# Decaying the samples' SSD states on ScalarE instead of GpSimd, in a one-core hybrid decoder step

## The reference, cut to what matters

```
dA_cs  = dt * A
state' = exp(dA_cs) * state  +  (dt * x)[p] * B[n]      # new state, an output (ssm_sample)
y[p]   = sum over n of state'[p, n] * C[n]              # goes on into the mixer's output
```

## Time and profile before

| | |
|---|---|
| median of three runs | 2261.55 us (2261.43 to 2262.20) |
| the profiled execution, its own time | 2264.14 us |
| the profiled execution, its span in the trace | 2262.4 us |
| PE busy | 2144.6 us, 95% of the span |
| DVE busy | 1173.7 us, 52% |
| ACT busy | 848.9 us, 38% |
| POOL busy | 126.5 us, 6% |
| mean granted clock of PE | 0.976 of full speed |

### The profile page before, as it was taken

How to read it: one execution, slowest core, us unless ns; L and a number is a source line. 1 busy time by engine, 2 the same in 40 slices (tenths; PEclk the granted TensorE clock), 3 DMA queues, 4 the chain that set the end, 5 groups by cost and what they waited for, 6 DMA issues and landing times.

```text
span 2262.4 us, 39108 instructions
## 1 busy us (share of the span) xinstructions
PE 2144.6 (95%) x17101; PEld 1972.2 (87%) x17101; DVE 1173.7 (52%) x1582; ACT 848.9 (38%) x1031; POOL 126.5 (6%) x146
## 2 busy tenths in 40 slices
PE   5699999999999999989988899999999999999997
PEld 1188999988999999889988898899999989999996
DVE  1454444444444445576788877444545434445555
ACT  0143333333333333355655443333333323333333
POOL 0000000000000000011567000000000000000000
PEclk9799999999999999999999999999999999999998
DMA  9988865778888657757454456865545688875552
GB/s 388 402 301 311 307 236 191 240 270 305 307 309 313 225 183 273 266 168 216 153 171 143 154 183 224 294 228 185 170 158 180 213 303 315 309 264 168 160 177 85
DMA packets 380761, 534.10 MB, mean 236 GB/s; under 512 B 11815, under 2 KB 356783, under 8 KB 357807
## 3 DMA queue, kind: packets, MB, share of 16 engines
q1 hardware_dynamic: 358288, 519.28, 66.2%
q10 hardware_dynamic: 22303, 12.33, 1.9%
HBM read 524.37 MB, written 7.19 MB: 235 GB/s over the span
## 4 chain that ended last, share of the span: by engine, by line
PE 81%; DMA 8%; DVE 7%; ACT 2%; issue 1%; POOL 1%; SPq 1%; ACTq 0%; DVEq 0%; POOLq 0%
PE main L1365 25%; PE main L1366 24%; PE main L1367 24%; DMA ada<-in_w_ada 7%; PE b L1329 6%; DVE w_lo L847 2%; DMA ada<-in_w_ada_f 1%; DVE ntile L903 1%; ACT w_hi L577 1%; DVE h_lo L898 0%; SPq L439 0%; PE b L1314 0%; DMA raw<-in_w_in 0%; DVE rec L1161 0%; POOL state L540 0%
## 5 line engine op out<-in xcount | busy, mean ns | idle before, releaser
L847 DVE TENSOR_TENSOR w_lo<-raw,w_hi 128x1024 fp32r<-128x1024 f32 (+2 forms) x720 | 798.3, 1114 | 927.5 <-ACT w_hi L577 925.7
L577 ACT ACTIVATE w_hi<-raw 128x1024 fp32r<-128x1024 f32 (+2 forms) x720 | 685.7, 956 | 1087.9 <-PE main L1367 1082.9
L1365 PE MATMUL main<-h_hi,w_hi 128*128 128x264 f32 x3664 | 1058.1, 289 | 21.6 <-DVE h_lo L898 7.9
L1366 PE MATMUL main<-h_lo,w_hi 128*128 128x264 f32 x3664 | 1050.5, 287 | 0.0
L1367 PE MATMUL main<-h_hi,w_lo 128*128 128x264 f32 x3664 | 1048.7, 286 | 0.0
L1365 PEld LDWEIGHTS main<-h_hi,w_hi 128*128 128x128 f32 x3664 | 698.5, 191 | 49.9 <-DVE w_lo L847 26.9
L1366 PEld LDWEIGHTS main<-h_lo,w_hi 128*128 128x128 f32 x3664 | 696.7, 190 | 0.4
L1367 PEld LDWEIGHTS main<-h_hi,w_lo 128*128 128x128 f32 x3664 | 696.4, 190 | 0.0
L1365 PE MATMUL main<-act_hi,w_hi 128*128 128x264 f32 x1408 | 402.2, 286 | 0.0
L1367 PE MATMUL main<-act_hi,w_lo 128*128 128x264 f32 x1408 | 400.4, 284 | 0.0
L1366 PE MATMUL main<-act_lo,w_hi 128*128 128x264 f32 x1408 | 399.9, 284 | 0.0
(11 more groups left out here) (213 smaller groups left out, 730.2 us busy)
## 6 DMA issues: line engine op xcount, KB each, us to landing
raw<-in_w_up SPq DMA_DIRECT2D x176, 1024.0 KB, 6.1
ada<-in_w_ada SPq DMA_DIRECT2D x144, 1024.0 KB, 9.2
raw<-in_w_down SPq DMA_DIRECT2D x96, 768.0 KB, 4.8
raw<-in_w_in SPq DMA_DIRECT2D x36, 1024.0 KB, 5.5
ada<-in_w_ada_f SPq DMA_DIRECT2D x32, 1024.0 KB, 10.6
raw<-in_w_down SPq DMA_DIRECT2D x32, 512.0 KB, 5.3
raw<-in_w_out SPq DMA_DIRECT2D x16, 1024.0 KB, 5.6
state<-in_state_ssm ACTq DMA_DIRECT2D x16, 256.0 KB, 4.0
```

The source lines that it names most:

```text
L577: A(split_view(w_hi, m, kind), raw_piece(m, kind), ACT.Copy).then_inc(hi_done, 1)
L847: TT(split_view(w_lo, m, kind), raw_piece(m, kind), split_view(w_hi, m, kind).bitcast(F32), ALU.subtract).then_inc(lo_done, 1)
L1365: MM(out, wh, hi[:, k, :], start=k == 0, stop=False)
L1366: MM(out, wh, lo[:, k, :], start=False, stop=False)
```

## The change

POOL's line 534 goes. ACT gets a function `state_decay(n)`, called in slot n as the last task of the slot: it waits until item n has landed (`st_in`), and then issues four activations of the form Copy with a scale, one for each of the item's four samples, in place, each on 128 x 128 with a scale read from one column of `dcs_f` (a value for each partition). The fourth raises the new semaphore `st_decayed`. POOL no longer waits for `st_in`; it makes the product with B first and waits for `st_decayed` ahead of the addition.

```diff
@@ -530,13 +531,12 @@
                 st, pr = state[:, i, :, :], prod[n % 2]
-                pool.wait_ge(st_in[i], 16 * (q + 1))
-                ch.link(pool.tensor_tensor(st, st, dcs_f[:, t, bs].unsqueeze(2).to_broadcast([P, 4, NSTATE]), ALU.mult))
                 pool.wait_ge(spread_done, 2 * q + 1)
                 if n >= 2:
                     pool.wait_ge(st_sum, n - 1)
                 ch.link(pool.tensor_tensor(pr, spread_b[:, :, :],
                                            xsdt[:, t, bs].unsqueeze(2).to_broadcast([P, 4, NSTATE]), ALU.mult))
+                pool.wait_ge(st_decayed, n + 1)
                 pool.tensor_tensor(st, st, pr, ALU.add).then_inc(st_new, 1)
@@ -666,6 +666,16 @@
+            def state_decay(n):
+                t, bs = item_place(n)
+                if n == 0:
+                    act.wait_ge(samp_placed, 1)
+                act.wait_ge(st_in[n % 4], 16 * (n // 4 + 1))
+                for b in range(4):
+                    ins_ = A(state[:, n % 4, b, :], state[:, n % 4, b, :], ACT.Copy,
+                             scale=dcs_f[:, t, bs.start + b:bs.start + b + 1])
+                ins_.then_inc(st_decayed, 1)
@@ -757,6 +767,8 @@
                 if kind == "lru" and j < 2:
                     spread_copy(2 * t + j, (spread_b, spread_c)[j][:, :, :])
+                if kind == "lru":
+                    state_decay(u)
```

More of the change, by code:

```diff
@@ L269, in build @@
         st_new, st_prod, st_sum = sem("st_new"), sem("st_prod"), sem("st_sum")
+        st_decayed = sem("st_decayed")
         z_tanh, sz_ready = sem("z_tanh"), sem("sz_ready")
```

## The result

The changed kernel takes 2269.55 us (median of 8 runs, 2264.20 to 2271.25), the kernel before 2261.99 us beside it on the same chip. The ratio is 1.0031, with a 95% interval of 1.0020 to 1.0042: the change makes the kernel slower, by 7.6 us between the medians. The span of the profiled execution grows from 2262.4 to 2268.3 us.

A forecast was written before the change was run, and what follows sets the result against it. PE was taken to wait on a chain over ACT and DVE until 1230.91 us, then to be the bound itself. Terms 3.75 + 0.2 + 1.4 + 1.2 - 2.4 + 0.6 = +4.75 gave 2266.3 us; range 2256.5 to 2273, the forecast's own 2263 to 2269.5.

The forecast's parts named there:

- step 2: Copies on the chain where DVE waits for w_hi: +3.75 us from slots 3, 7 and 11, +0.2 from slot 6.
- step 3: POOL's addition, waiting for the copies, and its product run into the w_lo pairs after slots 3, 7, 11: +1.4 us.
- step 4: DVE's steps on the chain, slots 4 to 14, no longer meet POOL's decay: -2.4 us together, bounds 0 and 7.1.
- Step 1: ACT's added work: four copies per item, about 394 ns each, 1.25 us together; 20 us for 16 items.
- Step 5: End of the stage, slot 15: copies and POOL's steps delay DVE 2.7 us, PE 2.1 us behind: +0.6 us.
- Step 6: The rest costs nothing: state loads issued two to three slots earlier, stores, ACT's queue, the wait for st_decayed, histories.
- A: Rival, chain through slots 4 to 14: DVE's relief outweighs the copies, 2258.4 or 2255.9 us; chance 0.25.
- B: Rival: longer PE waits bring one or two more clock falls on the chain, 2269.7 to 2273.1 us; chance 0.17.
- C: Rival: nothing moves, copies fall into ACT's waits and POOL's gain is taken up elsewhere, 2261 to 2262.5 us; chance 0.10.
- the rule on multiplications: The Trainium skill's advice to multiply on VectorE, not ScalarE; 16 products would put 9.6 us on DVE.

The follow-up runs named there:

- the third one: The changed kernel with item n's four copies at the start of slot n, behind its two w_hi pieces, instead of its end: 2257.66 us, 0.9979 against the kernel before.

## Why the prediction was right, and where only its sum was

The time (2269.55 us) lies in the range, the direction was the forecast's, and the mechanism of steps 2 and 3 stands in the trace. Against the runs beside it the loss is 7.6 us, interval 4.5 to 9.5, where I gave 4.75; the forecast's own range ended just below it, at 2269.5. That the sum fits is in part luck. Measured by themselves, its terms are two to six times as large and cancel: leaving the decay out gives back 8.1 us where step 4 has 2.4, on top of that the copies cost 8.5 us where step 2 has 3.95, and the wait in four items 7.8 us where step 3 has 1.4. In the kernel before, the copies of slots 3, 7, 11 and 15 cost only 1.1 us, so that step 2's price is no property of the copies alone.

The steps can be followed along the chain. Each number is the start or end of an event after, minus the same one before, minus the 0.72 us that this execution was already late at 1083 us:

| event | forecast | measured |
|---|---|---|
| end of slot 4's pair | +1.7 | +1.5 |
| start of slot 7's pair | +2.2 | +2.5 |
| end of slot 7's pair | +2.2 | +3.4 |
| start of slot 8's pair | +3.5 | +4.5 |
| start of slot 12's pair | +5.4 | +6.3 |
| end of slot 12's pair | +6.3 | +7.1 |
| start of slot 14's convolution | +4.9 | +3.3 |
| PE's return from the chain | +4.15 | +4.3 |
| end of the pair behind slot 15 | none given | +6.0 |
| PE behind the stage (line 1342, now 1354) | +4.75 | +4.85 |

**Step 1, right.** The 64 activations take 392 ns in the mean (estimated 394), four in a row 1.25 to 1.29 us.

**Step 2, right in the changed kernel's trace.** From the square root to slot 4's pair it is 1.63 us before and 2.80 after, +1.17; slot 8's pair moves by 1.1 us against the end of slot 7's (table).

**Step 3, right.** The three pairs take 3.76, 3.77 and 3.75 us (forecast 3.87). Against the earlier trace rows that is +0.31, -0.04 and +0.81, +1.1 us in all where I put +1.4.

**Step 4, right in its total on this chain, wrong in its parts and as a relief.** Line 987 (now 999) in slots 5 and 9 still takes 1.00 us and line 1169 (now 1181) of slot 13 fell to 0.70, as forecast. Two places went otherwise: slot 7's pair, which POOL had not lengthened, and the convolution of slot 14, where I took it that nothing of POOL moves up. The first two lines are the kernel before.

```profile
1152.39 1.22 POOL L552 COPY outcol<-rec 128x16 f32<-128x16 f32 x1
1153.56 2.02 POOL L534 TENSOR_TENSOR state<-state,dcs_f 128x512 f32<-128x512 f32 x1
...
1145.64 1.00 DVE L999 SCALAR_TENSOR_TENSOR cval<-cin,small,cfull 128x8 f32<-128x8 f32 x1
...
1155.55 3.20 DVE L859 TENSOR_TENSOR w_lo<-raw,w_hi 128x1024 fp32r<-128x1024 f32 x2
...
1226.42 0.70 DVE L1181 TENSOR_TENSOR out_l<-silu_g,rec 128x528 f32<-128x528 f32 x1
...
1232.36 2.78 DVE L990 SCALAR_TENSOR_TENSOR cfull<-cin,small,cfull 128x288 f32<-128x288 f32 x2
```

The prediction took POOL to be quiet beside slot 7's pair of the earlier trace rows. It was not: a small copy (0.21 us elsewhere) and a decay stood there, lengthened themselves, while the pair kept its 2.35 us. That a pair takes this long when POOL is quiet is right all the same (2.36 us at 1241.58). After, the pair takes 0.85 us more than in the earlier trace rows; the convolution, which I had falling to 1.1 us, takes 2.78, since the addition and the product (POOL, from 1232.10) had moved into the decay's place. Between the end of slot 12's pair and that convolution the chain gave back 3.8 us, where I had named 1.36 (0.86 and 0.5). So PE's return at +4.3 is right by errors that cancel.

As a price of the decay, the -2.4 us was mis-sized: without it and without anything in its place 8.1 us come back, more than the upper bound of 7.1. I had set the step against a POOL that waits for the copies, and so part of the relief was counted as "addition in place of decay" in step 3. The net came out near; the view that it gave was too small. It hid that a version which keeps POOL's steps in DVE's gaps gains, as the third one does.

**Step 5, near in its net, by two errors.** I gave the end of the stage 0.6 us, with 2.7 as the upper bound. Timeline of PE, first before, then after, from its return on:

```profile
1240.60 0.44 PE L1467 MATMUL b<-xdec,xdt 128*64 128x128 f32 x4
1247.65 0.44 PE L1467 MATMUL b<-xdec,xdt 128*64 128x128 f32 x4
...
1235.91 0.68 PE L1514 MATMUL b<-cval,gates_w 128*128 128x264 f32 x2 [1.91 <-issue]
1242.79 0.44 PE L1479 MATMUL b<-xdec,xdt 128*64 128x128 f32 x4
1248.49 0.39 PE L1377 MATMUL main<-h_hi,w_hi 128*128 128x264 f32 x1 [1.50 <-DVE w_lo L859]
1252.45 0.44 PE L1479 MATMUL b<-xdec,xdt 128*64 128x128 f32 x4 [0.76 <-DVE xdec L1058]
1253.97 0.36 PE L1377 MATMUL main<-h_hi,w_hi 128*128 128x264 f32 x1 [0.22 <-ACT silu_g L767]
```

Before, PE needs 9.69 us from its return (1230.91) to line 1467, with a clock of 0.51 in the first 5 us and 0.81 in the next; after, 6.88 us, with a clock of 1.00. That gives back 2.8 of the 4.3 us, and PE stands at +1.5. The forecast did not have this. Behind it PE waits 1.50 + 0.76 + 0.22 = 2.48 us where before it did not wait at all up to 1260 us, and where I had put below 1 us. DVE's delay came as forecast: from slot 15's square root (1239.96 before, 1244.10 after) to the end of the pair it is 1.18 + 1.40 = 2.6 us more, forecast 2.7. But the 2.1 us by which PE was behind DVE hold only for a PE that comes out of the slow stretch; without it PE is there 2.8 us sooner. With smaller gaps the waits make 3.4 us: the third item's matmul stands at 1254.70 before and 1260.28 after, +4.9, and line 1342 (now 1354) at 1296.75 and 1302.32, +4.85. Behind PE's return that is 0.6 us in all, the forecast's number, out of 2.8 us back and 3.4 us lost.

**Step 6, right.** No copy waited for its load (idle before the 64 copies 0.0 us). The working has the load two to three slots ahead; it is issued in the slot before, so nearly two.

**The rivals.** A named the relief and its size (7.1 us) nearly right, and did not come about, because the wait and the copies took it. The Trainium skill (SBUF — State Buffer, Who interferes with whom) speaks of an exclusive lock between the two engines; the trace agrees for single steps, 1.00 us where 0.23 would do. By that rule alone 16.6 us were to come back, and the kernel without decay gives 8.1: the three steps that stay move up and take part of the places. B did not come about, and its mechanism ran the other way at its place: behind PE's return the clock is 1.00 after and was 0.51 before. Another fall stands at 1210 to 1215 us instead (0.66), behind a wait of PE of 1.84 us for `w_lo` of slot 12; over 1130 to 1250 us the clock's loss is 0.17 of 40 us in both. C is excluded by the interval. As to the rule on multiplications, no run put the decay on DVE.

By PE's own steps the profiled execution is 0.7 us late ahead of the stage, 4.85 us in it and some 0.3 us behind it: 5.9 us, the difference of the two spans. The medians lie 7.6 us apart, since the profiled execution of the kernel before lay 2.15 us above its median and that of the change 0.45.

## What to carry to other kernels

Work taken off an engine that takes turns with the bound engine is worth what the steps that stay do next: look where they land, and leave out the old step with nothing in its place to see the whole of the gain. A new wait was dear here where its release comes at the same moment as the bound engine's own, the square root: with the new work a slot's length ahead of it, the waiting engine used the other's gaps again. The price of an added step on the chain is not a constant: the same four copies cost 1 us or 7, by whether a delay there is paid back elsewhere. And a sum that fits does not show that its terms do: here each of the three was two to six times too small.

## What the runs showed of the hardware

POOL is held up by DVE too, and in these two traces for longer than DVE by POOL. A single step of DVE is longer by at most 1.15 us (line 1177 at 1175.50 us, 1.32 us for 0.17). A product with B that takes 1.04 us undisturbed takes 4.15 us after, in the run of slot 14 in which DVE makes a pair and three steps on the prompt's state in a row. POOL's timeline there:

```profile
1227.87 4.15 POOL L537 TENSOR_TENSOR ntile<-spread_b,xsdt 128x512 f32<-128x512 f32 x1 [1.44 <-DVE samp L1072]
1232.10 1.29 POOL L540 TENSOR_TENSOR state<-state,ntile 128x512 f32<-128x512 f32 x1
1233.47 1.36 POOL L543 TENSOR_TENSOR ntile<-state,spread_c 128x512 f32<-128x512 f32 x1
```

The next product with B takes 2.71 us (1236.85 us) beside a pair that keeps its 2.35 us. Why POOL gets in between the two pieces of some pairs and not of these stays open; the profile's spans on POOL are rough.

Two waits of PE of much the same length at the same place, 1.68 us before and 1.91 us after, stand beside a clock of 0.51 (1.2 GHz) from 1230 to 1235 us in the one and of 1.00 (2.4 GHz) from 1235 to 1240 us in the other, with PE busy for 4.09 of 5 us in both. The wait alone does not decide it.
